# Expert weights of a fused two-block network: eight raw slots against four

## What is computed

```
def hier_moe(h, wg, bg, we, be, w_gate, w_up, w_down):
    t = h.reshape(-1, d_)
    ...
    gates = jnp.sum(jax.nn.one_hot(eid, N_EXPERTS) * weights[..., None], axis=1)
    y = jnp.zeros_like(t)
    for e in range(N_EXPERTS):
        act = jax.nn.silu(t @ w_gate[e]) * (t @ w_up[e]) * gates[:, e:e + 1]
        y = y + act @ w_down[e]
    return y.reshape(b_, s_, d_)
```

## Time and profile before

| | |
|---|---|
| median of 3 runs | 1643.65 us (1642.39 to 1644.24) |
| profiled execution | 1643.56 us, its span 1641.8 us, mean granted TensorE clock 0.995 |
| TensorE busy (matmul) | 1629.2 us, 99% of the span |
| VectorE, ScalarE, GpSimd busy | 1169.1, 900.3, 321.6 us |
| DMA | 301.57 MB, mean 184 GB/s |
| chain that ended last | TensorE 95%, VectorE 3%, ScalarE 1% |

### The profile page before, as it was taken

How to read it: one execution, slowest core, us unless ns; L and a number is a source line. 1 busy time by engine, 2 the same in 40 slices (tenths; PEclk the granted TensorE clock), 3 DMA queues, 4 the chain that set the end, 5 groups by cost and what they waited for, 6 DMA issues and landing times.

```text
span 1641.8 us, 33507 instructions
## 1 busy us (share of the span) xinstructions
PE 1629.2 (99%) x12520; PEld 1545.7 (94%) x12520; DVE 1169.1 (71%) x1960; ACT 900.3 (55%) x1466; POOL 321.6 (20%) x347
## 2 busy tenths in 40 slices
PE   9999999999999999999999999999999999999998
PEld 8998877899999998889999999999999888999998
DVE  7676899886665686767966657666568666887754
ACT  5467888854444565555544434444456555554543
POOL 1030222210001126333400010000103654520001
PEclk9998999999999999999999999999999999999999
DMA  8434999845455543434555555555555443555554
GB/s 288 144 121 179 365 343 366 311 146 178 168 173 173 170 163 117 142 104 155 191 169 177 166 180 175 170 178 169 178 162 173 130 142 116 180 195 188 180 182 139
DMA packets 88504, 301.57 MB, mean 184 GB/s; under 512 B 9552, under 2 KB 16720, under 8 KB 88016
## 3 DMA queue, kind: packets, MB, share of 16 engines
q1 hardware_dynamic: 84048, 295.93, 52.9%
q10 hardware_dynamic: 4352, 4.20, 0.8%
HBM read 298.74 MB, written 1.34 MB: 183 GB/s over the span
## 4 chain that ended last, share of the span: by engine, by line
PE 95%; DVE 3%; ACT 1%; issue 1%; DMA 0%; SPq 0%; DVEq 0%; ACTq 0%
PE PS L1118 25%; PE PS L1120 25%; PE PS L1119 25%; PE PS L1580 3%; PE PS L1581 3%; PE PS L1582 3%; DVE w_lo L1920 2%; PE PS L1723 2%; PE PS L1757 1%; PE PS L1731 1%; PE PS L1741 1%; PE PS L1761 1%; PE PS L1307 0%; PE PS L1537 0%; ACT w_hi L596 0%
## 5 line engine op out<-in xcount | busy, mean ns | idle before, releaser
L1920 DVE TENSOR_TENSOR w_lo<-raw,w_hi 128x1024 fp32r<-128x1024 f32 x486 | 615.8, 1275 | 199.2 <-ACT w_hi L596 138.9
L1118 PE MATMUL PS<-x_hi,w_hi 128*128 128x272 f32 (+1 forms) x2320 | 674.2, 291 | 2.0 <-DVE x_lo L1925 1.7
L1120 PE MATMUL PS<-x_hi,w_lo 128*128 128x272 f32 (+1 forms) x2320 | 665.6, 287 | 0.0
L1119 PE MATMUL PS<-x_lo,w_hi 128*128 128x272 f32 (+1 forms) x2320 | 663.3, 286 | 0.0
L1118 PEld LDWEIGHTS PS<-x_hi,w_hi 128*128 128x128 f32 x2320 | 437.8, 189 | 8.5 <-issue 5.0
L1119 PEld LDWEIGHTS PS<-x_lo,w_hi 128*128 128x128 f32 x2320 | 437.9, 189 | 0.3
L1120 PEld LDWEIGHTS PS<-x_hi,w_lo 128*128 128x128 f32 x2320 | 438.0, 189 | 0.0
L596 ACT ACTIVATE w_hi<-raw 128x1024 fp32r<-128x1024 f32 x326 | 339.9, 1054 | 142.8 <-PE PS L1120 125.5
L600 ACT ACTIVATE w_hi<-raw 128x1024 fp32r<-128x1024 f32 x160 | 169.6, 1060 | 227.0 <-PE PS L1120 227.0
L1118 PE MATMUL PS<-a_hi,w_hi 128*128 128x272 f32 (+1 forms) x1024 | 292.8, 286 | 0.0
L1120 PE MATMUL PS<-a_hi,w_lo 128*128 128x272 f32 (+1 forms) x1024 | 292.0, 285 | 0.0
(11 more groups left out here) (392 smaller groups left out, 1787.9 us busy)
## 6 DMA issues: line engine op xcount, KB each, us to landing
raw<-stream SPq DMA_DIRECT2D x486, 512.0 KB, 3.3
G<-stream SPq DMA_DIRECT2D x60, 512.0 KB, 5.4
biasB<-rpbz ACTq DMA_DIRECT2D x16, 256.0 KB, 3.1
G<-b1mats SPq DMA_DIRECT2D x2, 1024.0 KB, 7.9
raw<-stream SPq DMA_DIRECT2D x6, 256.0 KB, 5.9
h<-xT SPq DMA_DIRECT2D x4, 272.0 KB, 5.0
mat<-mats SPq DMA_DIRECT2D x1, 1080.0 KB, 7.7
out<-qk SPq DMA_DIRECT2D x3, 256.0 KB, 2.4
```

The costliest lines, as they stand in the source:

```text
L1118: pe.matmul(ps, hi, rh, start=first, stop=False)
L1119: pe.matmul(ps, hi, rl, start=False, stop=False)
L1120: return pe.matmul(ps, lo, rh, start=False, stop=last)
L1920: dve.tensor_tensor(w_lo[:, slot, :], raw_at(n) if isinstance(n, int) else raw[:, slot, :], w_hi[:, slot, :].bitcast(F32), ALU.subtract).t ...
```

## The change

All chunks use the four slots of `raw`. `raw_more`, its semaphores, `raw_at`, `raw_wait` and `RAW_LESS` are gone, and so are SP's two waits ahead of the first expert load. Every expert load waits for `w_lo` of chunk n-4. Line numbers of the new kernel are smaller: SP's expert loads are at L538, the splits at L569 and L1893.

```diff
-RAW_LESS = 16 * (MOE_C // RING - MOE_C // (2 * RING))
...
-        raw_more = [Gf[:, BW * i:BW * (i + 1)] for i in range(RING)]
...
-            sp.wait_ge(logits1_ready, 4 * HEADS1)
-            sp.wait_ge(misc_out, MISC_AT["conv"] + 1)
...
-                if i >= 2 * RING:
-                    sp.wait_ge(lo_done, n - 2 * RING + 1)
-                elif i >= RING:
-                    sp.wait_ge(lo_done, n - RING + 1)
+                sp.wait_ge(lo_done, n - RING + 1)
...
-                sp.dma_start(raw_at(n), src).then_inc(raw_more_landed[i % RING] if i % (2 * RING) < RING else raw_landed[n % RING], 16)
+                sp.dma_start(raw[:, n % RING, :], src).then_inc(raw_landed[n % RING], 16)
...
-                    raw_wait(act, n)
+                    act.wait_ge(raw_landed[slot], 16 * (n // RING + 1))
...
-                    act.activation(w_hi[:, slot, :], raw_at(n), ACT.Copy).then_inc(hi_done, 1)
+                    act.activation(w_hi[:, slot, :], raw[:, slot, :], ACT.Copy).then_inc(hi_done, 1)
...
-                dve.tensor_tensor(w_lo[:, slot, :], raw_at(n) if isinstance(n, int) else raw[:, slot, :],
+                dve.tensor_tensor(w_lo[:, slot, :], raw[:, slot, :],
```

More of the change, by code:

```diff
@@ L355, in build @@
         h_squared, rs_ready = sem("h_squared"), sem("rs_ready")
-        raw_more_landed = [sem(f"raw_more_landed{i}") for i in range(RING)]
         order_landed = sem("order_landed")
@@ L412, in slot_of @@
             return (base + c) % RING
[L414 to L431, removed]
         B2S = B1_CHUNKS % RING
@@ L592, in split_hi @@
                 if isinstance(n, int):
-                    raw_wait(act, n)
+                    act.wait_ge(raw_landed[slot], 16 * (n // RING + 1))
                     if n >= RING:
                         act.wait_ge(chunk_used, n - RING + 1)
-                    act.activation(w_hi[:, slot, :], raw_at(n), ACT.Copy).then_inc(hi_done, 1)
+                    act.activation(w_hi[:, slot, :], raw[:, slot, :], ACT.Copy).then_inc(hi_done, 1)
                 else:
-                    act.wait_ge(raw_landed[slot], 4 * n + (16 - 4 * slot - RAW_LESS))
+                    act.wait_ge(raw_landed[slot], 4 * n + (16 - 4 * slot))
                     act.wait_ge(chunk_used, n - (RING - 1))
```

## The result

| | before | after |
|---|---|---|
| median of the runs (4 each) | 1643.02 us | 1676.70 us |
| lowest to highest | 1641.86 to 1644.24 | 1675.84 to 1678.64 |
| ratio, 95% interval | | 1.021, 1.0197 to 1.0222 |
| profiled execution: time, span | 1643.56, 1641.8 | 1677.0, 1675.2 |
| mean granted clock | 0.995 | 0.995 |

The change costs 33.7 us between the medians and 33.4 between the profiled executions. The forecast was +29 us, 1673 us, with a range of 1656 to 1690.

What follows compares the result with a forecast made beforehand. TensorE was taken to bound the experts before, the four-slot ring of loads after: 108 x (1.76 - 1.485) = +29.7 us, less 1.5 at the tail, plus 0.7 for addresses, +29 us to 1673 us; range 1656 to 1690.

Steps and rivals of the forecast that it cites:

- What bounds before: Experts' stage before the change: runs at TensorE's pace, 1.485 us per chunk, with no wait for a DMA.
- The ring: Experts' loads: issue, landing, w_hi, w_lo shared by four chunks; (L + 2.55) / 4 = 1.76 us per chunk, L the landing.
- The landing: Expert load from issue to landing: taken as 4.5 us, between 4.2 and 4.7.
- The address in registers: Last 26 expert loads compute their address after the wait: 0.1 us each, a quarter per chunk, +0.7 us.
- The tail: End of the experts: TensorE done 1.4 us after w_lo instead of 2.97, giving back 1.5 us; turn and scatter stay.
- The start: First expert loads, up to chunk 37: changed waits even out, costed at nothing, with an uncertainty of 2 us.
- The sum: Whole kernel: +29.7 us for 108 chunks, +0.7, less 1.5, together +29 us, 1673 us.
- The signs by which I would tell: Experts' stage: landing median 4.2 to 4.7 us, 107 steps in 188 us, some 300 GB/s, splits waiting for DMA.
- A: Experts' loads: landing falls back to 3.3 us, the four slots keep pace, 1642 to 1646 us; chance 6%.
- B: Experts' stage: new gaps lower TensorE's clock; 140 us more, 1784 us, if throughout; chance 3%.
- C: Experts' start and stage: shorter queues land loads within 3.4 us, up to 4 us gained, 1640 us; chance 3%.
- D: Experts' loads: landing stays 5.3 us, +51 us, 1695 us; far end of the forecast's own case, no separate chance.

Runs made afterwards that it cites:

- e4: Kernel before with six slots instead of eight (two extra beside the four of raw), least recently used first: 1643.51 us, ratio 1.0006.
- e7: Four-slot kernel, each expert load bringing only half its columns (256 KB), splits and matmuls whole on partly stale data: 1644.12 us.
- e1: Kernel before with its eight slots kept, but each expert load waiting for w_lo of four chunks back: 1675.08 us in one run.
- e2: Four-slot kernel, each expert load after the fourth waiting for w_lo of chunk n-3 instead of n-4: 1725.55 us.
- e3: Kernel before with five slots instead of eight (one extra beside the four of raw), least recently used first: 1653.34 us, ratio 1.0075.
- e5: The four-slot kernel unchanged, run again as a comparison: 1680.72 us, ratio 1.022 against the kernel before.
- e11: Kernel before with six slots instead of eight and the 1080 KB table load moved behind the experts' last load: 1646.78 us, ratio 1.0020.
- e6: Four-slot kernel with ScalarE's act_T_out of the last expert unit moved ahead of w_hi of chunk 146: 1678.10 us, ratio 1.0208.
- e8: Kernel before, eight slots, with the 1080 KB table load moved from the expert loop to behind it: 1642.13 us, ratio 0.9992.

## Why the prediction was right

**What bounds before** was read rightly, TensorE and no load. e4 and e7 bring the pace back to 1.48 to 1.49 us by two different ways, and neither gets below it.

**The ring.** Its form held in every kernel that the ring bounds, to 0.04 us per chunk. R times the time per chunk, less the mean landing, is the ring's rest, which I had put at 2.55 us:

| kernel | R | us per chunk | mean landing | rest |
|---|---|---|---|---|
| after | 4 | 1.790 | 4.62 | 2.54 |
| e1 | 4 | 1.777 | 4.55 | 2.56 |
| e2 | 3 | 2.202 | 4.17 | 2.44 |
| e3 | 5 | 1.569 | 5.09 | 2.76 |

In after, 2.45 us lie between landing and the end of `w_lo`, and 0.06 between that and the next issue; the 0.03 that are missing to 2.54 are the two ends of the stretch, where the pace differs.

**The landing** is the term that was mis-sized. I took 4.5 us, between 4.2 and 4.7. The median is 4.5, but a ring turns by the mean, and that was 4.62: 0.12 / 4 = 0.03 us per chunk, 3.2 us over the stage. Of the 4.5 us that the sum of 28.9 lacked, the tail below has 1.7 and the address 0.3; the ring's rest of 2.54 and rounded terms take 0.7 back. The better choice lay in the rows: the seven loads of the earlier trace rows went out at one per 1.78 us, which is the pace the ring gives itself, and the turn of chunks 143 to 147 gave 1.78 outright.

**The address in registers** was +0.7 us. For chunks 38 to 119 the issue follows `w_lo` after 0.03 us in the mean, for the last 26 after 0.18. That is 26 x 0.15 / 4 = 1.0 us. Of the 26 only 24 compute their address: chunks 124 and 125 still belong to the fourth block and are issued after 0.03.

**The tail** was the step whose sign failed. I let TensorE be done 1.4 us after `w_lo` instead of 2.97, a gain of 1.5 us, and let the turn and the scatter behind it stay as they were. The lag did shrink: chunk 143's `w_lo` ends at 350.38 and its last matmul starts at 351.71. But the turn grew from 2.58 to 5.08 us, and the stage's +33.2 us (`w_lo` of 37 to that of 145) became +33.4 at TensorE's last expert matmul, so nothing was given back. TensorE waits 1.66 us for GpSimd's `qk` there, where its lag had hidden that before, and 0.70 for `a_lo`, whose input stands behind a split that now waits for its load. I had asked what is queued behind SyncE's waits, and not what is queued behind ScalarE's.

**The start** was taken as even within 2 us, and was, to 0.04 us. The closeness is luck: the same kernel in e5 had chunk 37's `w_lo` 2.7 us later, with more of the lower clock ahead of it, and e4 and e11, which had none of it in 149 to 156 us, had it at 159.8 and 159.1 us.

**The sum**: 29.7 and 0.7 less 1.5 became 33.2 for the stage and 0.2 behind it. The signs by which I would tell held: the median landing 4.5, 191.5 us for 107 steps against 188, about 300 GB/s, and the three waits in their order; TensorE's for `w_lo`, 29.1 / 108, are 0.27 us per chunk, where I had said about 0.3. Since the runs bear out the ring's terms one by one, the nearness of the sum is not luck; without the gain for the tail it would have been 30.4.

**The rivals.** *A*, a landing of 3.3 us: not even three slots and one load per 2.2 us brought it (4.17). The Trainium skill, page "SBUF — State Buffer", section "The DMA setup-cost knee", puts a DMA at a roughly fixed 2 us plus its bytes at 436 GB/s, from which 3.2 us is the estimate for 512 KB. The trace agrees where loads are 3 us apart, at 3.3, and not in the stage, where the mean was 4.2 to 5.2 with several under way. *B*, the clock: 1.00 through the stage in after; e5 and e6 have a single spell each, which I estimate at 1 to 2 us. *C*, faster: with a landing of 3.0 us (e7) the time was that of before, so there was nothing to gain behind the ring, and in e8 the gain of a lighter start, if there is one, is not told from none. *D*, 5.3 us: that belongs to a pace of 1.48; a ring that falls behind thins its own loads, and so gets a shorter landing.

## What to carry to other kernels

A prefetch ring of R slots turns in (landing + the rest of the ring) / R, and it is invisible until that passes the pace of the engine behind it: here 6 slots cost nothing that can be measured, 5 cost 10 us and 4 cost 34. Take the landing at the pace in question, as a mean, from a stretch of the trace that already runs so; the landing of a load by itself is too short. And when an engine begins to wait, look at what stands behind the waiting instruction in its queue: a small copy there can hold up a third engine.

## What was not expected of the hardware

The landing of a 512 KB load moves with how many are under way (mean landing over spacing): 1.1 under way 3.3 us, the median, 1.9 (e2) 4.2, 2.6 (after) 4.6, 3.2 (e3) 5.1, 3.5 (e4) 5.2. That feedback is mild: it takes some of the loss back, but a ring one slot shorter still lost 48.9 us more (e2 against after). 256 KB loads, 2.0 under way, took 3.0 us. Why e5 and e6 ran some microseconds longer than the first runs of after isn't settled as a whole. Both profiled executions had a mean landing of 4.70 us against 4.62 and one spell of the lower clock in the stage; in e5 2.7 of 4.8 us were lost ahead of it.
